# Log decays spread once, keys turned beside them, in the last chunk of a projection

## What is computed

```python
gc = jnp.cumsum(g, axis=-1)                     # g: log decay (B,H,N,64)
decay = jnp.exp(jnp.where(incl, gc[..., :, None] - gc[..., None, :], -jnp.inf))
k_beta = k * beta[..., None]
a_mat = jnp.where(strict, jnp.einsum('bhnid,bhnjd->bhnij', k_beta, k) * decay, 0.0)
lmat = a_mat + jnp.eye(C, dtype=a_mat.dtype)
sol = lax.linalg.triangular_solve(lmat, rhs, left_side=True, lower=True, unit_diagonal=True)
qk = jnp.einsum('bhnid,bhnjd->bhnij', q, k) * decay
q_dec = q * jnp.exp(gc)[..., None]
k_dec = k * jnp.exp(gc[..., -1:] - gc)[..., None]
g_tot = jnp.exp(gc[..., -1])
```

## Time and profile before

| | us |
|---|---|
| median of 3 runs | 1554.04 (1551.37 to 1554.55) |
| the profiled execution, whole | 1552.9 |
| its span, first to last instruction | 1551.1 |
| TensorE busy in it | 1489.2 (96%) |
| VectorE busy | 987.9 (64%) |
| ScalarE busy | 797.1 (51%) |
| GpSimd busy | 126.1 (8%) |

### The profile page before, as it was taken

The page is one execution under the profiler, slowest core; times in us unless marked ns, Lnnn a source line. Parts: engine busy times, 40 slices in busy tenths (PEclk is TensorE's granted clock), DMA queues, the critical chain, the costliest instruction groups (busy, mean ns, idle before and its releaser), DMA issues.

```text
span 1551.1 us, 38390 instructions
## 1 busy us (share of the span) xinstructions
PE 1489.2 (96%) x15697; PEld 1218.9 (79%) x15697; DVE 987.9 (64%) x1374; ACT 797.1 (51%) x1014; POOL 126.1 (8%) x70
## 2 busy tenths in 40 slices
PE   7998999999999999999999999989999999999998
PEld 6997877899999989999999899966555455555554
DVE  3497434176666366765634645667787787888786
ACT  4447216344333358644132445465767576676664
POOL 0321500000433000000311000000000000000000
PEclk9999999999999999999999999999999999999999
DMA  8556265745555535553113334469999999999994
GB/s 277 180 177 210 92 204 169 266 147 170 177 186 190 178 123 163 163 163 109 57 56 109 109 117 163 137 267 348 409 399 397 370 404 414 416 415 387 416 415 190
DMA packets 178595, 362.26 MB, mean 234 GB/s; under 512 B 9229, under 2 KB 137722, under 8 KB 161658
## 3 DMA queue, kind: packets, MB, share of 16 engines
q1 hardware_dynamic: 178426, 359.90, 64.0%
HBM read 355.03 MB, written 1.05 MB: 230 GB/s over the span
## 4 chain that ended last, share of the span: by engine, by line
PE 71%; DVE 6%; DMA 6%; ACT 4%; issue 2%; DVEq 1%; ACTq 0%; SPq 0%; POOLq 0%
PE psum L3295 9%; PE psum L371 8%; PE psum L372 8%; PE psum L375 8%; DMA proj<-in_w_exp_up 5%; PE psum L3311 5%; PE psum L696 4%; PE psum L3348 3%; PE psum L568 3%; PE psum L3266 2%; PE psum L504 2%; PE psum L505 2%; PE psum L506 2%; PE psum L546 1%; DVE ring L2519 1%
## 5 line engine op out<-in xcount | busy, mean ns | idle before, releaser
L371 PE MATMUL psum<-proj_r 128*128 128x256 f32 x1392 | 342.7, 286 | 4.0 <-ACT proj_r L335 3.9
L372 PE MATMUL psum<-proj_r 128*128 128x256 f32 x1392 | 339.9, 284 | 0.0
L340 DVE TENSOR_TENSOR ring_r<-ring,proj_r 128x2048 fp32r<-128x2048 f32 x94 | 226.4, 2410 | 158.5 <-ACT proj_r L335 157.8
L2519 DVE COPY ring<-proj 128x1024 f32 x374 | 237.2, 688 | 91.2 <-POOLq L1424 47.3
L371 PEld LDWEIGHTS psum<-proj_r 128*128 128x128 f32 x1392 | 269.0, 193 | 8.0 <-issue 7.0
L372 PEld LDWEIGHTS psum<-proj_r 128*128 128x128 f32 x1392 | 269.0, 193 | 0.1
L335 ACT ACTIVATE proj_r<-ring 128x2048 fp32r<-128x2048 f32 x93 | 177.6, 1909 | 103.3 <-PE psum L375 93.0
L1884 ACT ACTIVATE ring<-proj 128x1024 f32 x186 | 189.1, 1051 | 6.8 <-issue 6.2
L375 PE MATMUL psum<-proj_r,ring_r 128*128 128x256 f32 x1392 | 182.9, 285 | 2.6 <-DVE ring_r L340 2.6
L375 PEld LDWEIGHTS psum<-proj_r,ring_r 128*128 128x128 f32 x1392 | 174.7, 194 | 3.0 <-DVE ring_r L340 2.8
L3295 PE MATMUL psum<-ring,u 128*32 128x256 f32 x1488 | 114.7, 385 | 3.3 <-DVE ring L2519 2.3
(11 more groups left out here) (570 smaller groups left out, 2707.3 us busy)
## 6 DMA issues: line engine op xcount, KB each, us to landing
ring<-in_w_in SPq DMA_DIRECT2D x65, 1024.0 KB, 5.3
proj<-in_w_exp_gate SPq DMA_DIRECT2D x64, 1024.0 KB, 9.4
proj<-in_w_exp_up SPq DMA_DIRECT2D x64, 1024.0 KB, 10.3
proj<-in_w_exp_down SPq DMA_DIRECT2D x64, 1024.0 KB, 8.1
ring<-in_w_ada SPq DMA_DIRECT2D x24, 1024.0 KB, 7.8
ring<-in_w_ffn_in SPq DMA_DIRECT2D x22, 1024.0 KB, 5.1
ring<-in_w_ffn_out SPq DMA_DIRECT2D x11, 1024.0 KB, 4.9
ring<-in_w_out SPq DMA_DIRECT2D x8, 1024.0 KB, 5.0
```

Of the source, the lines that this page charges most:

```text
L340: dve.tensor_tensor(ring_r[:, at.slot, :], ring[:, at.slot, :], self.heads[at.buffer].bitcast(F32), ALU.subtract) \
L371: pe.matmul(dst, w, xh, start=start, stop=False, skip_group_check=True)
L372: pe.matmul(dst, w, xl, start=False, stop=False, skip_group_check=True)
L2519: ins = dve.tensor_copy(into_copy[k_half][j][:, kind * D:(kind + 1) * D], pieces[:, bass.ds((piece + kind) & 7, 1), of_half].rearrange("p ...
```

## The change

Four things move, and one is dropped.

- The log decays are spread once, for all 256 tokens of each head (`gc_all`, 256 columns per head, two heads to a bank, banks 2 to 5), and within chunk 25: after every four fp32r matmuls with heads stands one spreading matmul. The second spreading (32 matmuls of 64 columns, L3018 before) is dropped.
- The transposes of the keys go into chunk 25 too, those of tokens 0 to 127 ahead of its first matmul, those of tokens 128 to 191 between its matmuls with heads and those with rests. Both now use banks 6 and 7, so the second waits until VectorE has read the first (`kd_made`).
- VectorE makes `decays` from `gc_all` ahead of the barrier, in four subtractions of 64 partitions each (heads 0 to 3 and then 4 to 7, each half of the partitions by itself) and two additions of the mask. `keys_ready` is raised in chunk 24.
- ScalarE takes the exponential `eg` in two instructions, heads 4 to 7 and then 0 to 3, each while VectorE reads the other banks, ahead of copying out chunk 25. The exponentials of `decays` come ahead of the barrier too.
- The products of keys wait for single banks: 0 and 1 for the copies of chunks 24 and 25, 2 and 3 until `gc_all` has been read.

```diff
@@ ScalarE, chunk 25 and behind it
                 if c == PROJ_2 - 1:
                     aside.head(act, 1)
+                    act.wait_ge(*reached("gc_all_spread", 1))
+                    act.activation(eg[:, 4:8, :], gc_all[:, 4:8, HD:S], ACT.Exp).then_inc(sig("eg_ready"), 1)
+                    act.wait_ge(*reached("gc_read", 1))
+                    act.activation(eg[:, 0:4, :], gc_all[:, 0:4, HD:S], ACT.Exp).then_inc(sig("eg_ready"), 1)
                 act.wait_ge(multiplied, at.n + 1)
...
-            act.wait_ge(*reached("gc_all_spread", 1))
-            act.activation(eg.rearrange("p (b h) t -> p b (h t)", b=4), psum[:, 2:6, 0:384], ACT.Exp).then_inc(sig("eg_ready"), 1)
-            act.wait_ge(*reached("eg_ready", 1))
-            for c in range(2):
-                act.activation(chunk_decay[:, c, :], eg[:, :, HD * (c + 1) - 1], ACT.Copy)
-            st.end()
...
                 act.activation(flat_pair(decays[:, ch]), flat_pair(decays[:, ch]), ACT.Exp).then_inc(sig("decay_exp"), 1)
+            act.wait_ge(*reached("eg_ready", 2))
+            for c in range(2):
+                act.activation(chunk_decay[:, c, :], eg[:, :, HD * (c + 1) - 1], ACT.Copy)
+            st.end()
@@ VectorE, behind the rests of the first chunk aside
+            decayed_keys(0)
+            aside.rest(dve, 1)
+            dve.wait_ge(*reached("gc_all_spread", 1))
+            for hh in range(2):
+                heads = slice(4 * hh, 4 * hh + 4)
+                if hh:
+                    dve.wait_ge(*reached("eg_ready", 1))
+                for be in range(2):
+                    part = slice(HD * be, HD * be + HD)
+                    ins = dve.tensor_tensor(decays[part, :, heads, :], gc_all[part, heads, :].rearrange("p h (c b t) -> p c h b t", c=TB, b=2)[:, :, :, be, :],
+                                            gc_col[part, :, heads].rearrange("p c (h o) -> p c h o", o=1).to_broadcast([HD, TB, 4, HD]), ALU.subtract)
+                ins.then_inc(sig("gc_read"), 1)
+            dve.wait_ge(*reached("gc_read", 2))
+            for ch in range(TB):
+                dve.tensor_tensor(decays[:, ch], decays[:, ch], spread(const("half_causal"), GH), ALU.add).then_inc(sig("decay_log"), 1)
+            decayed_keys(1)
             st.end()
@@ TensorE, chunk 25
+                elif c == PROJ_2 - 1:
+                    turn_keys(0)
+                    pe.wait_ge(hi_made, at.split + 1)
+                    for hd in range(GH):
+                        heads_by(pe, split_in_2, at, products[2 * hd:2 * hd + 2])
+                        last = row_to_all(pe, gc_all[:, hd, :], gc_rows, hd, GH)
+                    last.then_inc(sig("gc_all_spread"), 1)
+                    turn_keys(1)
+                    pe.wait_ge(lo_ready, at.split + 1)
+                    rests_by(pe, at, products).then_inc(multiplied, 1)
@@ TensorE, behind the barrier
-                last.then_inc(sig("gc_spread"), 1)
-            for ch in range(TB):
+                if ch == 1:
+                    pe.wait_ge(*reached("gc_read", 2))
+                    pe.wait_ge(*reached("eg_ready", 2))
```

More of the change, by code:

```diff
@@ L2267, in _, with decayed_keys @@
             aside.rest(dve, 0)
[L2268 to L2271, removed]
-            for ch in range(TB):
+            def decayed_keys(ch):
                 part = slice(0, P if ch == 0 else HD)
                 dve.wait_ge(*reached("gk_turned", ch + 1))
-                dve.tensor_tensor(kd_tok[part, ch], psum[part, 6 - 6 * ch:8 - 6 * ch, :].rearrange("p b (h n) -> p (b h) n", n=P),
-                                  kd_col[part, 8 * ch:8 * ch + 8].rearrange("p (h o) -> p h o", o=1).to_broadcast([part.stop, GH, P]), ALU.mult)
@@ L2277, in _ @@
-            st.end()
-            for ch in range(TB):
-                dve.wait_ge(*reached("gc_spread", ch + 1))
-                link(dve.tensor_tensor(decays[:, ch], bank[4 + ch].rearrange("p (h t) -> p h t", h=GH),
-                                       gc_col[:, ch, :].rearrange("p (h o) -> p h o", o=1).to_broadcast([P, GH, HD]), ALU.subtract))
-                dve.tensor_tensor(decays[:, ch], decays[:, ch], spread(const("half_causal"), GH), ALU.add).then_inc(sig("decay_log"), 1)
+                dve.tensor_tensor(kd_tok[part, ch], psum[part, 6:8, :].rearrange("p b (h n) -> p (b h) n", n=P),
+                                  kd_col[part, 8 * ch:8 * ch + 8].rearrange("p (h o) -> p h o", o=1).to_broadcast([part.stop, GH, P]), ALU.mult) \
+                   .then_inc(sig("kd_made"), 1)
@@ L2291, in _ @@
                 g_solver.begin(dve, link, ch)
-            dve.wait_ge(*reached("eg_ready", 1))
+            dve.wait_ge(*reached("eg_ready", 2))
             for ch, t0, e0 in ((0, HD, 0), (1, 0, HD)):
@@ L2951, in turn_values, with turn_keys @@
                 last.then_inc(sig("gv_turned"), 1)
+            def turn_keys(ch):
+                n = P if ch == 0 else HD
+                if ch == 0:
+                    pe.wait_ge(*reached("vb_ready", 2))
+                    pe.wait_ge(*reached("keys_ready", 1))
+                else:
+                    pe.wait_ge(*reached("kd_made", 1))
+                for hd in range(GH):
+                    last = pe.transpose(bank[6 + hd // 4][0:n, hd % 4 * P:(hd % 4 + 1) * P], proj[:, T_GK + hd, ch * P:ch * P + n], ident)
+                last.then_inc(sig("gk_turned"), 1)
             for c in range(PROJ_2):
@@ L3014, in _ @@
             for ch in range(TB):
+                if ch == 1:
+                    pe.wait_ge(*reached("gc_read", 2))
+                    pe.wait_ge(*reached("eg_ready", 2))
                 for hd in range(GH):
-                    for be in range(2):
-                        part, tok = slice(HD * be, HD * be + HD), ch * P + HD * be
-                        last = pe.matmul(bank[4 + ch][part, hd * HD:(hd + 1) * HD], ident[0:GH, hd:hd + 1].to_broadcast([GH, HD]),
-                                         gc_rows[:, tok:tok + HD], start=True, stop=True)
-                last.then_inc(sig("gc_spread"), 1)
-            for ch in range(TB):
-                for hd in range(GH):
+                    if ch == 0 and hd % 4 == 0:
+                        pe.wait_ge(evacuated, place.linear + 1 + hd // 4)
                     for be in range(2):
@@ L3027, in _ @@
                 last.then_inc(sig("g_prods_made"), 1)
+            pe.wait_ge(*reached("kd_made", TB))
             aside.multiply(pe, DIL_FRONT)
```

21 lines of the change are left out of this document (8 added, 13 removed).

## The result

| us | before | changed |
|---|---|---|
| median of 20 runs each | 1554.19 (1550.32 to 1558.2) | 1561.09 (1554.11 to 1569.29) |
| profiled execution, whole | 1552.9 | 1559.3 |
| its span | 1551.1 | 1557.3 |

The ratio is 1.0045, with a 95% interval of 1.0033 to 1.0056. That is slower by more than the 0.2% that can be told apart, and outside the predicted range of 1550.9 to 1557.9.

The account below looks back on a forecast made before the run. TensorE, working or waiting, was taken to bound the kernel. The terms summed to 26.9 us at half clock in the key products against 26.41, 0.5 us more: 1554.5 us, range 1550.9 to 1557.9.

Parts of the forecast that it names:

- (a): Eight key transposes ahead of chunk 25's matmuls on TensorE: 1.0 us.
- (b): Chunk 25's matmuls with heads on TensorE: 3.84 us, as before.
- (d): Changes between fp32r and float32 matmuls in chunk 25: 16 at 0.11 us, 1.8 us, bounds 0 and 3.6.
- (e): VectorE from the spreading to the barrier: four subtractions, two additions, `kd_tok`, handing over and gaps, 5.7 us.
- (j): Behind the barrier: second spreading gone, 2.16 us less; first half of key products 3.46 us at half clock, 1.65 at full.
- C: Rival: chunk 25's mixed stretch is too light for full clock; +2.2 us with one dip, +3.9 with two; chance 0.15.
- (f): TensorE behind the spreading: transposes and rests 3.0 us, then idle some 2.7 us until VectorE is done.
- (g): ScalarE's exponentials and copy of the chunk before the barrier: about 5.5 us, just under VectorE's 5.7.
- (c): Spreading of 256 instead of 192 columns in chunk 25: 3.72 us.
- (h): Second transposes' wait for `kd_made`: no cost, VectorE being done about 7 us before TensorE asks.
- (i): SyncE's load and DMA issued later, by 8 us and 2 to 3 us: nothing waits for either.

Follow-up runs that it names:

- the version in one piece: Changed kernel with its eight 8-row spreading matmuls together behind the 32 matmuls with heads; 1556.1 us, ratio 1.0004 to the kernel before.
- the version with the spreading first: Changed kernel with 128-row spreading ahead of the matmuls with heads, ScalarE's exponentials ahead of its copy of chunk 25; 1551.93 us, ratio 0.9985.
- 128 rows: Changed kernel with the interleaved spreading matmuls taken over 128 rows instead of 8; 1553.45 us, ratio 0.9993 to the kernel before.
- one piece, 128 rows: Changed kernel with the spreading matmuls together behind the matmuls with heads and over 128 rows; 1552.84 us, ratio 0.999 to the kernel before.
- 32 rows: Changed kernel with the interleaved spreading matmuls taken over 32 rows instead of 8; 1558.09 us, ratio 1.0022 to the kernel before.
- the repetition: The changed kernel, unaltered, measured and traced once more; 1561.88 us, ratio 1.0044 to the kernel before.

## Why the prediction was wrong

**What bounds the kernel** held: the time went by TensorE and what it waits for in this stretch. It grew by 5.0 us in the trace; the medians differ by 7, so some 2 us of the difference aren't located.

**The sum, by its terms.** Forecast 26.9, measured 31.55.

| term | forecast us | measured us |
|---|---|---|
| (a) eight transposes | 1.0 | 0.8 |
| (b) to (d) mixed stretch, 727.46 to 740.98 | 9.4 | 13.5 |
| (e) to the barrier and the key products, to 747.23 | 5.7 | 6.25 |
| (j) first half of the key products | 3.56 | 3.73 |
| VectorE's last products and beginnings | 7.28 | 7.26 |

**(d), changes of kind: too small, and for another reason.** At 1.8 us I took 0.11 for each change, from L504 and L505. Without any such cost a piece would be (3.84 + 3.72) / 8 = 0.94 us; with full rows, turns included, it took 0.90. So turns between fp32r and float32 alone cost nothing that shows. With 8 rows it is 1.29: 0.39 more for a piece, 3.1 us for eight instead of the 1.8 added. The row I chose has weights of 128 rows and could not show this. The upper bound of 3.6 us had it in, and the words beside it ("the weights of 8 rows to wait for") named the cause, which I gave no weight.

**The choice among the rivals: this decided it.** I took full clock in the chunk and gave C, the mixed stretch too light, 0.15. C occurred, in both traces that were taken of the changed kernel. What spoke for it stood in the earlier trace rows: 2.60 us of 8-row matmuls, TensorE busy in all of it, and 0.50 behind. I set against it that more than half of the stretch was full matmuls. That was an argument without a row, and it is the step that failed: full matmuls in between did not keep the clock up.

**C's price was too small.** I had 1.7 us for a dip, and room for two with full clock between, +3.9 in all. There was nothing between: once at 0.50 the mixed stretch stayed there to its end, and the fall lasted 10.2 us in one trace and 13.7 in the other. Three pieces at 2.30 us instead of 1.29 are 3.0 us of the 4.1 by which the mixed stretch was too short; most of the rest is (d). Behind it the transposes and rests, at 0.50 and partly so, took 4.3 us for the 3.0 of (f), of which 0.55 us shows on the way to the key products. In both traces the clock did not come back while light work went on, so the price of a fall was not that of one row of the old trace.

**(e), (f) and (g).** Each of VectorE's durations came out as forecast. Timeline of VectorE, changed kernel:

```profile
741.01 2.81 DVE L2292 TENSOR_TENSOR extra<-psum,small 64x512 f32<-64x512 f32 x4 [9.42 <-PE psum L1135]
743.86 1.30 DVE L2297 TENSOR_TENSOR extra<-extra,cst 128x512 f32<-128x512 f32 x2
745.19 1.22 DVE L2279 TENSOR_TENSOR work<-psum,small 64x1024 f32<-64x1024 f32 x1
```

Four subtractions at 0.70 (forecast 0.69), two additions at 0.65, `kd_tok` 1.22. But who was last was wrong: the transposes and rests, slowed by the clock, ended later, so ScalarE's copy of the chunk began at 745.32 and ScalarE came last to the barrier. The gap was 1.95 us instead of 2.7. I had set ScalarE 0.2 us under VectorE, and said that "nothing there costs more"; that held only at full clock.

**(c), (h) and (i)** held: 3.65 us for 3.72 in the version in one piece; the first keys were turned and multiplied by about 729 (VectorE's product began at 727.95), and no wait of TensorE for them shows.

**(j)**: one fall behind the gap, 3.73 us for 3.56, as forecast in this trace; in the other trace it did not come, so that this term came out is partly luck. The untouched 7.28 us measured 7.26.

**The chances** don't quite add up: the parts give 0.06 for faster and 0.83 for the same, where 0.07 and 0.82 are written. The result doesn't hang on it.

**The rules weighed.** On the mixed stretch the Trainium skill ("TensorE: Matmul & The Clock Gate", section "What's actually happening"), by which the clock follows how busy TensorE has been, speaks for full clock; the traces disagree: busy 6.70 of 6.70 us at 0.50. The same page (section "Part 4: PE-mode transpose") has it that transposes don't count as busy in the same way, which the prediction took to mean a fall in the chunk from those that were moved; moved alone, they kept 1.00 (7.40 of 7.40 us busy).

**Open.** Why the version with the spreading first, with a stretch 5 us shorter, gains only about 2 us (interval 0 to 4.7). And what decides whether the key products fall behind the gap: gaps of 1.95 us (changed, and spreading in one piece) and 2.75 us (128 rows) were followed by 0.50; gaps of 2.74 us (one piece, 128 rows) and 2.63 us (32 rows), and the 1.95 us of the repetition, were not. Numbers of rows between 8 and 32, and between 32 and 128, were not tried.

## What to carry to other kernels

A matmul whose weights fill few rows was dear twice here: standing among full ones it cost 0.39 us each time for the turn (8 and 32 rows), and with 8 rows it pulled TensorE's clock down on itself and on what followed. Where a selection or a broadcast is done by matmul, try it with all 128 rows, zeros in the weights where a row doesn't count and finite numbers in the data there: the matmuls took no longer for it, and here that alone, without any reordering, made the kernel 0.3 to 0.4% faster. Before moving such work in between other work, ask of each row of the old trace with a lowered clock what ran just ahead of it, since that will now run ahead of something else, and for longer.

## What the runs showed that I had not expected

- **8 rows lower the clock, 32 don't, in the same place.** With 8 rows the mixed stretch went at 0.50 from 733.7 to its end at 741.0 in one trace and from 732.3 to 740.6 in the other; with 32 and with 128 rows (one trace each) it kept 1.00 throughout. What sets in with 8 rows doesn't do so at once: the first 6 us or so of the stretch still had full clock.
- **Partly filled rows cost a turn.** 0.39 us for a piece of four full matmuls and one with 8 or with 32 rows (1.29 against 0.90 us), at full clock. In one piece, without turns, the 16 records of 256 columns took 3.65 us with 8 rows and 3.47 with 128 (of 192 columns 2.79 and 2.60).
- **The clock can stay low under constant work.** TensorE was busy 7.80 of 7.80 us on the mixed work and 5.10 of 5.10 us on full-row work behind it, both at 0.50, in the repetition.
